# A decoder layer on one core: the mixer norm's root row spread by two transfers instead of TensorE, two reorderings on VectorE, and GpSimd multiplying two blocks of the last output half

## What is computed

```python
x = x + 0.5 * swiglu(rmsnorm(x, ffn1_norm), ffn1_w_gate, ffn1_w_up, ffn1_w_down)
h = rmsnorm(x, mix_norm)                 # the second norm: y * rsqrt(mean(y*y) + EPS) * g
proj = h @ w_in                          # q | k | v | o | i,f gates | pool channels
qk = silu(causal_dwconv(proj[q, k]))     # four taps along the sequence
gates = proj[i, f] + b_gates             # feed cumulative sums and maxima along the sequence
hm = mlstm_chunkwise(q, k, v, gates)     # then a norm for each head, times sigmoid(o)
hp = multiscale_pool(proj[pool])
x = x + concat(hm, hp) @ w_out
x = x + 0.5 * swiglu(rmsnorm(x, ffn2_norm), ffn2_w_gate, ffn2_w_up, ffn2_w_down)
return rmsnorm(x, final_norm)
```

## Time and profile before

| | |
|---|---|
| median of 3 runs | 895.78 us (895.74 to 896.03) |
| the profiled execution's own time | 896.22 us |
| its span (first to last instruction) | 894.4 us |
| PE busy | 887.2 us (99%) |
| DVE busy | 673.8 us (75%) |
| ACT busy | 450.1 us (50%) |
| POOL busy | 42.7 us (5%) |

### The profile page before, as it was taken

One profiled execution on the slowest core, in us unless ns is written; L12 is line 12 of the kernel. 1 busy time (PEld: TensorE's weight loads), 2 busy tenths in 40 slices (PEclk: granted clock), 3 DMA queues, 4 the chain that ended last, 5 costly groups with the idle time before them and its releaser, 6 DMA issues.

```text
span 894.4 us, 15568 instructions
## 1 busy us (share of the span) xinstructions
PE 887.2 (99%) x5572; PEld 804.4 (90%) x5572; DVE 673.8 (75%) x1158; ACT 450.1 (50%) x753; POOL 42.7 (5%) x63
## 2 busy tenths in 40 slices
PE   9999999999999999999999999999999999999997
PEld 7899999999988888888888888999999999888887
DVE  7999999999553534677886699899999998534334
ACT  7665666666432323444853374666666665323221
POOL 0000000000000000001435100000000000000000
PEclk9999999999999999999999999999999999999999
DMA  6233333332523332223323232333323332433312
GB/s 247 94 116 98 97 112 104 110 94 70 177 104 108 100 111 95 93 72 107 107 72 99 83 125 71 107 106 111 100 95 111 100 114 84 136 113 99 112 48 95
DMA packets 39420, 93.84 MB, mean 105 GB/s; under 512 B 4436, under 2 KB 5092, under 8 KB 39384
## 3 DMA queue, kind: packets, MB, share of 16 engines
q1 hardware_dynamic: 39064, 92.83, 31.7%
q0 software_dynamic: 176, 0.46, 0.2%
q10 hardware_dynamic: 144, 0.08, 0.0%
HBM read 91.24 MB, written 2.11 MB: 104 GB/s over the span
## 4 chain that ended last, share of the span: by engine, by line
PE 95%; DVE 3%; ACT 1%; issue 1%; DMA 0%; DVEq 0%; SPq 0%; ACTq 0%
PE ps L414 16%; PE ps L416 16%; PE ps L415 16%; PE ps L519 14%; PE ps L521 14%; PE ps L520 13%; PE ps L444 1%; PE ps L447 1%; PE ps L450 1%; DVE w_lo L1426 1%; PE ps L465 0%; PE ps L820 0%; PE ps L674 0%; PE ps L682 0%; DMA raw<-weights 0%
## 5 line engine op out<-in xcount | busy, mean ns | idle before, releaser
L1309 DVE TENSOR_TENSOR w_lo<-raw,w_hi 128x1024 fp32r<-128x1024 f32 x83 | 101.6, 1224 | 118.7 <-ACT w_hi L845 112.9
L414 PE MATMUL ps<-act_hi,w_hi 128*128 128x512 f32 (+1 forms) x470 | 178.7, 380 | 0.0
L416 PE MATMUL ps<-act_hi,w_lo 128*128 128x512 f32 (+1 forms) x470 | 178.2, 379 | 0.0
L415 PE MATMUL ps<-act_lo,w_hi 128*128 128x512 f32 (+1 forms) x470 | 178.2, 379 | 0.0
L519 PE MATMUL ps<-xg_hi,w_hi 128*128 128x256 f32 x608 | 174.1, 286 | 0.3 <-DVE work L1462 0.3
L521 PE MATMUL ps<-xg_hi,w_lo 128*128 128x256 f32 x608 | 172.2, 283 | 0.0
L520 PE MATMUL ps<-xg_lo,w_hi 128*128 128x256 f32 x608 | 171.9, 283 | 0.0
L845 ACT ACTIVATE w_hi<-raw 128x1024 fp32r<-128x1024 f32 x75 | 79.0, 1056 | 150.9 <-PE ps L416 146.0
L519 PE MATMUL ps<-xe_hi,w_hi 128*128 128x256 f32 x456 | 128.0, 281 | 0.0
L521 PE MATMUL ps<-xe_hi,w_lo 128*128 128x256 f32 x456 | 127.2, 279 | 0.0
L520 PE MATMUL ps<-xe_lo,w_hi 128*128 128x256 f32 x456 | 127.2, 279 | 0.0
(11 more groups left out here) (221 smaller groups left out, 1377.9 us busy)
## 6 DMA issues: line engine op xcount, KB each, us to landing
raw<-weights SPq DMA_DIRECT2D x85, 512.0 KB, 3.3
raw<-weights SPq DMA_DIRECT2D x152, 256.0 KB, 2.7
x<-x_t SPq DMA_DIRECT2D x8, 256.0 KB, 6.0
first<-weights SPq DMA_DIRECT2D x8, 256.0 KB, 5.7
work<-neg_rows SPq DMA_DIRECT2D x4, 256.0 KB, 3.2
root<-root_rows SPq DMA_DIRECT2D x4, 256.0 KB, 3.8
out<-sums SPq DMA_DIRECT2D x3, 256.0 KB, 2.1
out<-raw SPq DMA_DIRECT2D x3, 256.0 KB, 2.2
```

Of the source, the lines that this page charges most:

```text
L414: pe.matmul(acc, hi, m_hi, start=first, stop=False)
L415: pe.matmul(acc, hi, m_lo, start=False, stop=False)
L416: return pe.matmul(acc, lo, m_hi, start=False, stop=last)
L1309: dve.tensor_tensor(w_lo[:, k % SLOTS], raw[:, k % RAWS], f32(w_hi[:, k % SLOTS]), ALU.subtract).then_inc(lo_made, 1)
```

## The change

It has four parts. In the mixer TensorE no longer spreads the root columns: it turns them once, inside the first q/k unit (`turn_norm`), ScalarE copies the four rows out (`turn_norm_out`), and SyncE writes and reads them back onto all partitions into `rinv` (`spread_norm`), between the loads of units MIX+5 and MIX+6. VectorE's copy goes; it waits for the transfer instead, and has the unit's low part ahead of that wait. Next, in the later turns of the mixer loop VectorE does `gates_second` before the low part of the turn, scales the last q/k unit one turn earlier, right behind the one before it, and does its taps before it waits for the gate columns. In each FFN the second `iteration` does `product` before `sum_4`. Last, blocks 4 and 5 of the second output half go to GpSimd, from a copy of the root row that VectorE makes after its first product.

```diff
-LAST_STORES = ((0, 1), (1, 1), (2, 2), (4, 2), (6, 2))
+LAST_STORES = ((0, 1), (1, 1), (2, 2), (6, 2))
+POOL_STORE = (4, 2)
 # SyncE
+            def spread_norm(i):
+                sp.wait_ge(norm_turned, i + 1)
+                sp.dma_start(norm_rows[i].rearrange("(b p) -> b p", p=P),
+                             (turned, mask)[i][0:TB]).then_inc(norm_out, 16)
+                sp.wait_ge(norm_out, 16 * (i + 1))
+                sp.dma_start(rinv[:], norm_rows[i:i + 1].partition_broadcast(P)).then_inc(norm_in, 16)
-            units(DN1 + RAWS, MIX + 15)
+            units(DN1 + RAWS, MIX + 6)
+            spread_norm(0)
+            units(MIX + 6, MIX + 15)
...
+            d, n = POOL_STORE
+            sp.wait_ge(ya_made, KD - FIRST_DVE + n)
+            sp.dma_start(out[1, :, d:d + n], y_half[1][:, d:d + n]).then_inc(stored, 16)
 # TensorE
+            def turn_norm(stage):
+                pe.wait_ge(col_step, STEPS * (stage + 1))
+                pe.transpose(ps[0:TB, 7, 0:P], ycol[:], ident[:]).then_inc(rep_made, 1)
...
+                    if k == KD - 1:
+                        turn_norm(1)
...
-                        if i == 0:
-                            replicate(1)
 # ScalarE
+            def turn_norm_out(i):
+                act.wait_ge(rep_made, i + 2)
...
+                act.activation((turned, mask)[i][0:TB], ps[0:TB, 7, 0:P], ACT.Copy).then_inc(norm_turned, 1)
 # GpSimd
+            pool.wait_ge(half_rinv, 1)
+            for d in range(POOL_STORE[0], sum(POOL_STORE)):
+                pool.wait_ge(gained, d + 1)
+                pool.tensor_tensor(y_half[1][:, d], x[:, d, HALF:T], rinv[:, HALF:T], ALU.mult).then_inc(ya_made, 1)
 # VectorE, FFN (second is true in the second iteration only)
+                    if second:
+                        product(s - 1, 1 - par)
+                    if not tail:
                         sum_4(s + 1)
-                    if not head:
+                    if not head and not second:
                         product(s - 1, 1 - par)
 # VectorE, mixer
-                take_rinv(1)
...
+                    split_next()
                     dve.wait_ge(g_sum, 2)
+                    norm_spread(0)
...
                     if pending is not None:
                         taps(pending)
+                    if n == V_UNIT[1]:
+                        gates_second()
+                    if n == QK_UNIT[6]:
+                        scaled(7)
+                        taps(6)
...
-                    if n == V_UNIT[1]:
-                        gates_second()
+                taps(7)
                 dve.wait_ge(cols_made, 1)
                 dve.tensor_copy(cols[:], ps[:, 3, 0:2 * TB * HEADS]).then_inc(cols_made, 1)
-                taps(7)
                 qk_lo(6)
+                qk_lo(7)
                 split_next()
-                qk_lo(7)
 # VectorE, the last output half
+                    if d == 0:
+                        dve.tensor_copy(rinv[:, at], ps[:, 6, at]).then_inc(half_rinv, 1)
```

More of the change, by code:

```diff
@@ L105, with build_layer @@
 S_COLS = 1280
-def build_layer(nc, weights, pool_w, x_t, vecs, consts, neg_rows, root_rows, out):
+def build_layer(nc, weights, pool_w, x_t, vecs, consts, neg_rows, root_rows, norm_rows, out):
     ctx = ExitStack()
@@ L239, in build_layer @@
         half_made, qsq_made = sem("half_made"), sem("qsq_made")
+        norm_turned, norm_out, norm_in = sem("norm_turned"), sem("norm_out"), sem("norm_in")
         turn_made, root_out, root_in = sem("turn_made"), sem("root_out"), [sem(f"root_in{i}") for i in range(2)]
@@ L248, in build_layer @@
         gained, last_rinv, ya_made = sem("gained"), sem("last_rinv"), sem("ya_made")
+        half_rinv = sem("half_rinv")
         yb_made, root_made = sem("yb_made"), sem("root_made")
@@ L551, in period @@
                     if head:
-                        pe.wait_ge(rinv_made, stage + 1)
+                        pe.wait_ge(rinv_made, 1 + p)
                     else:
@@ L1053, in last_gains @@
                         act.preload_act_table_set("sqrt_and_others")
+            def turn_norm_out(i):
+                act.wait_ge(rep_made, i + 2)
+                if i >= 1:
+                    act.wait_ge(root_out, 16 * HEADS)
+                act.activation((turned, mask)[i][0:TB], ps[0:TB, 7, 0:P], ACT.Copy).then_inc(norm_turned, 1)
             def mixer():
@@ L1064, in mixer @@
                 act.preload_act_table_set("natural_log_exp_and_others")
+                turn_norm_out(0)
                 fr = slice(32, 32 + HEADS)
@@ L1149, in turn_out @@
                         act.wait_ge(root_out, 16 * h)
+                    else:
+                        act.wait_ge(norm_out, 16)
                     act.activation(turned[0:TB], ps[0:TB, 7, 0:P], ACT.Copy).then_inc(turn_made, 1)
@@ L1359, in inverse_rms, with norm_spread @@
                     dve.tensor_copy(rcol[:], ycol[:])
+            def norm_spread(i):
+                dve.wait_ge(norm_in, 16 * (i + 1))
             def take_rinv(stage):
@@ L1363, in take_rinv @@
                 dve.tensor_copy(rinv[:], ps_rep).then_inc(rinv_made, 1)
-                dve.wait_ge(rinv_made, stage + 1)
+                dve.wait_ge(rinv_made, 1 + stage // 2)
             def terms(p, k):
@@ L1474, in corner_22, with iteration @@
                     dve.tensor_tensor(u_half[1], ps_b[par], p5_sb[par], ALU.add).then_inc(c22_made, 1)
-                def iteration(s, par, head=False, tail=False):
+                def iteration(s, par, head=False, tail=False, second=False):
                     if not tail:
@@ L1566, in ffn_up @@
                 iteration(0, 0, head=True)
-                iteration(1, 1)
+                iteration(1, 1, second=True)
                 with dve.Fori(1, NSP[p] // 2 - 1) as it:
@@ L1667, in taps, with scaled @@
                     ins.then_inc(conv_done, 1)
+                def scaled(i):
+                    dve.wait_ge(unit_used, QK_UNIT[i] + 1)
+                    dve.tensor_tensor(work[:, i % 2], ps[:, qk_bank[i % 3]], rinv[:], ALU.mult).then_inc(u_made, 1)
                 def qk_lo(i):
@@ L1675, in mixer @@
                 gates_in()
-                split_next()
                 pending = None
                 for n in range(MIX + 1, V_UNIT[2]):
-                    if n in QK_UNIT:
+                    if n in QK_UNIT and n < QK_UNIT[7]:
                         i = QK_UNIT.index(n)
-                        dve.wait_ge(unit_used, n + 1)
-                        dve.tensor_tensor(work[:, i % 2], ps[:, qk_bank[i % 3]], rinv[:], ALU.mult).then_inc(u_made, 1)
+                        scaled(i)
                     if pending is not None:
                         taps(pending)
+                    if n == V_UNIT[1]:
[3 more added lines that the diff above has]
+                        taps(6)
                     if n < QK_UNIT[7]:
@@ L1688, in mixer @@
                             qk_lo(pending)
-                    pending = i if n in QK_UNIT else None
+                    pending = i if n in QK_UNIT and n < QK_UNIT[6] else None
                     if n == V_UNIT[0]:
                         gates_first()
-                    if n == V_UNIT[1]:
-                        gates_second()
+                taps(7)
                 dve.wait_ge(cols_made, 1)
                 dve.tensor_copy(cols[:], ps[:, 3, 0:2 * TB * HEADS]).then_inc(cols_made, 1)
-                taps(7)
                 qk_lo(6)
+                qk_lo(7)
                 split_next()
-                qk_lo(7)
                 dve.wait_ge(cols_made, 3)
@@ L1992 @@
     root_rows = nc.dram_tensor("root_rows", (HEADS, T), F32, kind="Internal").ap()
-    build_layer(nc, *args, neg_rows, root_rows, out)
+    norm_rows = nc.dram_tensor("norm_rows", (2, T), F32, kind="Internal").ap()
+    build_layer(nc, *args, neg_rows, root_rows, norm_rows, out)
     r = run_bass_kernel_spmd(nc, [arrays], core_ids=[0])
```

2 lines of the change are left out of this document (1 added, 1 removed).

## The result

| | before | changed |
|---|---|---|
| median of the runs, us | 895.78 (894.97 to 896.03, 10 runs) | 897.65 (897.00 to 899.31, 10 runs) |
| ratio, 95% interval | | 1.0023 [1.0015, 1.0031] |
| profiled execution, span | 894.4 | 895.8 |

The prediction was 895.3, with a range up to 896.3. It was wrong: the changed kernel is slower by about 1.9 us. The two profiled spans differ by 1.4 us, and that part can be laid out place by place.

What follows compares the result with a forecast made beforehand. The prediction took TensorE's own matmul stream to bound the kernel, with only 1.7 us of waits. Mixer -0.78, FFNs 0 and end +0.33 sum to -0.45, so 895.78 becomes 895.3 us, range 894.6 to 896.3.

Steps and rivals of the forecast that it cites:

- The mixer's stream, -0.78: Mixer, TensorE: four spreading matmuls of 0.89 us become one turn of 0.11, saving 0.78, bounds 0.7 to 0.9.
- The root's arrival and what waits behind it: Mixer: root lands at 368.7, 3.3 us later; first scaling starts 0.8 late at 370.4, low part near 373.5.
- From there on what TensorE waits for is started by TensorE's own results, so it moves along. I take the whole 0.78.: After `values(0)`: the mixer's whole 0.78 us saving survives to the end; 0.20 is left if the reordering fails.
- that meeting of the two engines only at the end: Rival at the last output half: GpSimd and VectorE get into each other's way, 896.1 us; chance 0.06.
- The late root costs TensorE nothing.: Mixer: slack of 5.4 us before MIX+5 and 3.5 before the fourth q/k unit covers the later root; cost 0.
- In the second FFN `product` is not what TensorE waits for there ... so again nothing.: Second FFN: `product` ahead of `sum_4` changes nothing, as rows 1 list no such wait of TensorE.
- The end, +0.33: Last output half: third store waits 0.33 us longer behind the copy, so the end costs 0.33, bounds 0.2 to 0.6.
- the rule that the prediction set against this: Last stores: about 2.0 us fixed plus bytes at 436 GB/s each; the end would cost 0.2 us, not 0.33.
- The first FFN: TensorE's 0.32 us wait before the second iteration's period moves by one period; cost nothing, bounds 0 and 0.5 gained.
- The sum of -0.45: Whole kernel: -0.78 for the mixer, 0 for the FFNs and +0.33 for the end make 0.45 us less.
- the mixer's saving is lost later: Rival, at `values(0)` or where another engine does not follow: 0.20 of 0.78 us is left, 895.9; chance 0.12.

Runs made afterwards that it cites:

- e9: e8 plus two warm-up products cut into eight more matmul pieces; 895.81 us against 896.36 for the kernel before, ratio 1.0002.
- e16: Kernel before plus root by transfers, new mixer order, one idle 256 KB transfer and eight more warm-up pieces; 896.73 us against 896.08, ratio 1.0013.
- e5: Kernel before plus one VectorE copy (about 0.6 us) ahead of the second FFN's second iteration; 896.43 us against 895.62, ratio 1.0011.
- e7: Kernel before plus the root's two transfers, on idle buffers, at their place in SyncE's queue; 896.60 us against 895.62, ratio 1.0010.
- e11: Kernel before plus one idle 2 KB transfer onto all partitions in SyncE's queue; 897.29 us against 896.36, ratio 1.0009.
- e2: Kernel before plus only `product` ahead of `sum_4` in both FFNs' second iteration; 896.46 us against 896.51, ratio 1.0000.
- e4: Changed kernel with two warm-up products cut into eight more matmul pieces; 898.98 us against 896.51 for the kernel before, ratio 1.0026.
- e8: Kernel before plus root by transfers, issued by GpSimd instead of SyncE, and new mixer order; 896.56 us against 895.62, ratio 1.0008.
- e1: Kernel before plus only the GpSimd part of the last output half; 897.04 us against 896.51, ratio 1.0003.
- e18: Changed kernel plus idle transfer, eight warm-up pieces and VectorE waiting for the first head's key sums; 896.00 us against 895.96 before, ratio 1.0004.
- e13: Kernel before plus two idle 256 KB transfers onto all partitions in SyncE's queue; 896.18 us against 896.08, ratio 1.0000.
- e10: Kernel before plus only the small idle write to DRAM in SyncE's queue; 896.37 us against 896.36, ratio 1.0000.
- e3: Changed kernel without its end and FFN parts: root by transfers and new mixer order; 898.13 us against 896.51 for the kernel before, ratio 1.0016.
- e14: Changed kernel plus one idle 256 KB transfer behind the root's read-back; 897.40 us against 896.08 for the kernel before, ratio 1.0016.
- e17: e16 plus VectorE waiting for the first head's key sums before two low parts; 897.12 us against 895.96 for the kernel before, ratio 1.0009.

## Why the prediction was wrong

**The mixer's stream, -0.78.** Right: 0.79 by the rows, 0.11 for the turn, and in e9 the matmul at the start of the second FFN comes 188.7 us after the mixer's first (542.14 and 353.46), against 189.5 before.

**The root's arrival and what waits behind it.** Right within 0.3 us at each step, and no wait of TensorE; `probs_lo` was done at 433.1 and `values(0)` began at 435.55, forecast by 434 and at 435.7.

**"From there on what TensorE waits for is started by TensorE's own results, so it moves along. I take the whole 0.78."** This step failed, twice. Behind it stood the reading of rows 1 with which the prediction begins, that almost all of the time is TensorE's own stream.
- At the first head the exponentials wait for GpSimd. With VectorE's work earlier, GpSimd's sums fell beside VectorE operations with two inputs in SBUF, and 3.8 us became 5.6: 0.6 of 0.78 went there. I had weighed that meeting of the two engines only at the end, where it did not happen. The rule of the Trainium skill ("SBUF — State Buffer", Who interferes with whom), that such a VectorE instruction and a GpSimd instruction that reads SBUF exclude each other for a whole instruction, is what e16's copy shows (0.30 to 1.57 us), and the addition behind the copy in the changed kernel (1.04 to 2.25). At the end, with the root read from PSUM, GpSimd's two products took 1.41, undisturbed, by the same rule.
- In the second FFN TensorE's place is set by VectorE's loop and its block loads. That loop ran 10.11 us a period (151.7 / 15), TensorE's own 10.02 (599.05 to 609.07), and the 0.77 in hand near 599 was gone by 679. An earlier TensorE gains nothing there; a later loop costs its lateness (e5). With the change the loop was 0.67 late near 599 and 1.14 near 750.

**"The late root costs TensorE nothing."** Right for the root, wrong for its transfers. The read-back costs 0.9 to 1.0 us by the medians (e7, e11). The traces show 0.8 and 0.6 of it in the second FFN's loop, where the block load that releases `sum_1` takes longer. No row of the kernel before shows that, but I set the price of two more transfers at nothing, with no bound, because their queue had time.

**"In the second FFN `product` is not what TensorE waits for there ... so again nothing."** The swap did cost nothing (e2). The reason given was unsound: the product is 0.77 ahead near 599 and 0.13 from 679 on, where it is the bound, and the list of waits shows none of it.

**The fetch.** Seven matmul pieces fewer in TensorE's stream moved an instruction fetch from 560.5 to 561.7, into the first block loads; `sum_1` began 0.77 late. This was in no step. Moving it back removed the wait (e4, e9), and with the transfers on GpSimd's queue the medians went from 0.9 over the kernel before (e8) to 0.55 under it (e9), though neither ratio is clear of 1.

**The end, +0.33.** Measured 0.26 in the changed kernel and 0.3 in e1, inside its bounds, and the last landing came 0.27 later, forecast 0.3. The last issue was 0.11 later and not 0.2; the third store, which the sum went by, was 0.33 later. The Trainium skill gives the rule that the prediction set against this ("DMA: Bandwidth & Descriptors", Anatomy of one DMA), a fixed time plus the bytes for each transfer, for transfers that GpSimd issues; these are SyncE's. Here a last store of the same size took 2.28 us from issue to landing before and 2.44 with the change; by the last issue alone the end would have cost 0.11. **The first FFN**: the wait moved by one period, as forecast.

**The size.** The sum of -0.45 became +1.4 in the profile: 0.6 at the head and, in the second FFN, 1.5. The runs say +1.9: the traced execution of the kernel before was 0.44 above its median (896.22), that of the changed kernel at its median. The three causes each show in traces and go with their repair; in the medians all three repairs together (e18) take the loss from 1.9 to nothing, but the forecast gain does not appear, since four of eleven executions lie in the upper group, whose cause stays open. By themselves the swap and the order cost nothing and the end its 0.3; the loss comes with the root. Of the rivals "the mixer's saving is lost later" named the mechanism, and its 895.9 left out that the loss can be more than the saving.

## What to carry to other kernels

Before costing a saving in one stage, measure for each later stage who paces it, by comparing the producer's end and the consumer's start in an early and a late period, not by the list of waits. When work moves on VectorE, look at what GpSimd does at the new time and whether both read SBUF. And a transfer that nobody waits for, or a few matmuls fewer, can still move later transfers: give such edits a bound of about 0.1% on a kernel of this kind, and test with an idle copy of the transfer.

## What the hardware showed that I had not expected

- One transfer of 2 KB onto all partitions, put into SyncE's queue some 200 us ahead of a loop of block loads and waited for by nobody, lengthened the load that releases each period by some 0.04 us (2.54 to 2.58; load waits 4.3 to 4.8 us over 16) and the kernel by 0.9 us by the medians (e11); two of them did nothing (e13: 3.8 us, +0.1), nor did a small write (e10: +0.0). On GpSimd's queue the load waits were 3.7 (e8) and 4.5 (e9).
- A fetch of TensorE's instructions (0.02 MB on the instruction queue) that ran beside two 256 KB loads made them take 3.4 to 4.1 us (changed, e3, e8, e14) instead of 2.5 to 3.1, and where it falls depends on how many instructions TensorE has had before: eight pieces more in the warm-up moved the fetch from 561.7 (changed) to 560.0 (e4), and from 562.1 (e8) to 559.8 (e9).
- With GpSimd's and VectorE's SBUF reads side by side, GpSimd's sums went from 3.8 to as much as 6.1 us (e14 to e16), and VectorE's two low parts from 2.4 (e17) to 3.7 us (changed).
